# Routed experts: tokens fetched and results sent by indirect transfers, in place of products with a selection matrix, with the weights in rings of four buffers

## What is computed

```python
def moe_swiglu(x, router_w, router_b, w13, w2):
    t = x.reshape(b * n, d)
    logits = (t @ router_w).astype(jnp.float32) + router_b.astype(jnp.float32)
    probs = jax.nn.softmax(logits, axis=-1)
    top_p, top_i = lax.top_k(probs, TOP_K)
    top_p = top_p / jnp.sum(top_p, axis=-1, keepdims=True)
    gates = jnp.einsum('tk,tke->te', top_p, jax.nn.one_hot(top_i, N_EXPERTS, dtype=jnp.float32))
    out = jnp.zeros_like(t)
    for e in range(N_EXPERTS):
        out = out + gates[:, e:e + 1] * swiglu(t, w13[e], w2[e])
    return out.reshape(b, n, d)
# then: x = x + g2 * out; y = rmsnorm(x, final_norm)
```

## Time and profile before

| | us |
|---|---|
| median of 3 runs | 3472.29 (3462.05 to 3472.33) |
| the profiled execution | 3476.86 |
| its span, first to last instruction | 3475.1 |
| TensorE busy | 3105.1 |
| VectorE busy | 1412.7 |
| GpSimd busy | 1125.0 |
| ScalarE busy | 868.6 |

### The profile page before, as it was taken

One profiled execution on the slowest core, in us unless ns is written; L12 is line 12 of the kernel. 1 busy time (PEld: TensorE's weight loads), 2 busy tenths in 40 slices (PEclk: granted clock), 3 DMA queues, 4 the chain that ended last, 5 costly groups with the idle time before them and its releaser, 6 DMA issues.

```text
span 3475.1 us, 51066 instructions
## 1 busy us (share of the span) xinstructions
PE 3105.1 (89%) x20356; PEld 2801.9 (81%) x20356; DVE 1412.7 (41%) x1999; ACT 868.6 (25%) x1266; POOL 1125.0 (32%) x365
## 2 busy tenths in 40 slices
PE   7699888888888887899999896769999999999996
PEld 3499787777777775799999896768888888888895
DVE  0400246555654654421111406434444544453454
ACT  0200122322232222110010100123333334333432
POOL 1255022012202212456566454213323333332330
PEclk9799677677767866899999998869999999999997
DMA  9233211101110110122222121014545455454542
GB/s 297 84 128 107 70 34 55 40 24 45 39 48 21 54 51 26 49 61 83 57 74 72 57 82 51 10 49 128 145 139 163 137 142 155 139 139 145 161 137 71
DMA packets 427939, 309.93 MB, mean 89 GB/s; under 512 B 12145, under 2 KB 393066, under 8 KB 427882
## 3 DMA queue, kind: packets, MB, share of 16 engines
q1 hardware_dynamic: 414698, 286.08, 27.9%
q10 hardware_dynamic: 13184, 23.07, 1.9%
HBM read 294.96 MB, written 14.16 MB: 89 GB/s over the span
## 4 chain that ended last, share of the span: by engine, by line
PE 36%; issue 31%; POOL 12%; DVE 4%; ACT 2%; DMA 1%; DVEq 0%; POOLq 0%; SPq 0%; ACTq 0%
PE psum L542 15%; POOL m_lo L392 9%; PE psum L525 7%; PE psum L684 2%; PE psum L701 2%; PE psum L676 2%; POOL w_hi L433 2%; PE psum L691 2%; PE psum L590 2%; PE psum L707 1%; POOL w_lo L436 1%; DVE xt L1395 1%; PE psum L794 1%; ACT vn L1002 1%; PE psum L520 1%
## 5 line engine op out<-in xcount | busy, mean ns | idle before, releaser
L392 POOL TENSOR_TENSOR m_lo<-m_raw,m_hi 128x2048 fp32r<-128x2048 f32 (+1 forms) x81 | 357.3, 4411 | 724.9 <-ACT m_hi L1124 724.9
L778 PE MATMUL psum<-he_hi,m_hi 128*128 128x192 f32 x1584 | 444.1, 280 | 17.9 <-POOL m_lo L392 16.4
L433 POOL TENSOR_TENSOR w_hi<-raw,zero 128x2048 fp32r<-128x2048 f32 (+2 forms) x68 | 249.3, 3667 | 648.5 <-PE psum L542 549.4
L778 PE MATMUL psum<-he_lo,m_hi 128*128 128x192 f32 x1584 | 441.4, 279 | 0.0
L778 PE MATMUL psum<-he_hi,m_lo 128*128 128x192 f32 x1584 | 441.1, 278 | 0.0
L542 PE MATMUL psum<-a_hi,w_hi 128*128 128x320 f32 x1728 | 398.7, 312 | 42.8 <-DVE cy L1514 17.1
L542 PE MATMUL psum<-a_lo,w_hi 128*128 128x320 f32 x1728 | 397.6, 312 | 0.0
L542 PE MATMUL psum<-a_hi,w_lo 128*128 128x320 f32 x1728 | 397.1, 311 | 0.0
L469 POOL TENSOR_TENSOR ml<-lt,level 128x640 f32<-128x640 f32 x80 | 124.0, 1556 | 795.4 <-PE psum L525 795.1
L1124 ACT ACTIVATE m_hi<-m_raw 128x2048 fp32r<-128x2048 f32 (+1 forms) x164 | 290.5, 1772 | 345.6 <-DMA m_raw<-in_moe_w_dram 260.8
L436 POOL TENSOR_TENSOR w_lo<-raw,w_hi 128x2048 fp32r<-128x2048 f32 (+2 forms) x68 | 333.6, 4906 | 5.3
(11 more groups left out here) (297 smaller groups left out, 5217.5 us busy)
## 6 DMA issues: line engine op xcount, KB each, us to landing
m_raw<-in_moe_w_dram SPq DMA_DIRECT2D x274, 512.0 KB, 4.5
raw<-in_mod_w_dram SPq DMA_DIRECT2D x48, 512.0 KB, 3.9
raw<-in_ffn_w_dram SPq DMA_DIRECT2D x44, 512.0 KB, 4.7
mod_raw<-in_mod_w_dram SPq DMA_DIRECT2D x16, 1024.0 KB, 6.9
raw<-in_dn_w_in_dram SPq DMA_DIRECT2D x32, 512.0 KB, 4.5
m_raw<-in_moe_w_dram SPq DMA_DIRECT2D x54, 256.0 KB, 2.7
raw<-in_sc_w_in_dram SPq DMA_DIRECT2D x24, 512.0 KB, 4.1
projected<-stage ACTq DMA_DIRECT2D x16, 640.0 KB, 3.1
```

What stands on the lines that cost most here:

```text
L392: eng.tensor_tensor(m_lo[q][:, 0:n], m_raw[j % 2][:, 0:n], m_hi[q][:, 0:n].bitcast(F32), ALU.subtract)\
L433: pool.tensor_tensor(w_hi[s][:, 0:cols], raw[s][:, 0:cols], zero[:, :].broadcast_to([P, cols]), ALU.add)\
L778: mm = pe.matmul(psum[:, q, g * CAP:(g + 1) * CAP], w[:, c:c + P], v[:, k, :], start=(k == 0 and n == 0), stop=(k == KT - 1 and n == 2))
```

## The change

Nothing of what is computed changes. In the expert stage:

- `h_rows` in DRAM takes the normed tokens row by row. TensorE turns them back with 16 fp32r products for each of five tiles (high and low added in PSUM), ScalarE copies and sends them from its own queue. `xT` is turned back too, by 40 transposes, into `xtok2`.
- A table in DRAM has for each item and slot the token's row, the output row and the gate. GpSimd fills it with default entries (four `iota`, two memsets, two plain transfers of 16-byte pieces), VectorE computes `dest` and the gates by twelve small steps, GpSimd writes the entries by ten indirect transfers, waits, reads the whole table back (2880 pieces of 16 bytes in two plain transfers) and waits. Then it issues the first gather, sets `yb` to zero and gives the count that the first even weight loads wait for.
- In the loop GpSimd issues, before the low half of unit 10, two indirect transfers that send the previous item's output rows `yb` to `y_rows` and two that fetch the next item's token rows to `xg`. TensorE turns `xg` by 16 transposes at the place of the gather. Scatter, way back, `pick`, `back`, `y_hi`, `y_lo` and the additions to `xT` are gone; the output is scaled into `yb` by ScalarE alone.
- The weights have rings of four (`m_raw`, `m_hi`, `m_lo`); ScalarE makes high halves three units ahead. The down matrix is cut into nine units (seven single, two double), so an item has 20. An up unit is still three products of 192 for each tile, gate and up part now in different banks.
- At the end SyncE reads each token's two output rows (5 transfers of 1 MB); VectorE adds them, scales them by the gate row, adds `xtok2`; ScalarE makes sum of squares and root; VectorE scales; SyncE sends each tile.
- Several semaphores of earlier stages are merged; their waits stay as they are.

The diff, cut to its core:

```diff
-SLOTS = [(0, 0, P), (1, P, CAP - P)]
+PARTS = [(0, 0, P), (1, P, CAP - P)]
-DOWN_K = [(0, 1), (1, 1), (2, 1), (3, 2), (5, 2), (7, 2), (9, 2)]
+DOWN_K = [(k, 1) for k in range(7)] + [(7, 2), (9, 2)]
+RING = 4
+AHEAD = 3
...
@@ SyncE
+            for w in range(2):
+                sp.dma_start(g2_row[w].rearrange("(k p) -> p k", p=P), mod[:, 40:48, w],
+                             allow_slow_non_contiguous=True).then_inc(sem("g2_out"), 16)
...
+            def m_load(x, j, dst_src):
+                sp.wait_ge(sem(f"m_split{j % 2}"), x * (M_UNITS // 2) + (j // 2 + 1))
+                for dst, src in dst_src:
+                    sp.dma_start(dst, src).then_inc(sem(f"m_loaded{j % RING}"), 16)
...
@@ GpSimd
+            def gather_rows(idx):
+
+                for i, s0, ns in PARTS:
+                    pool.indirect_dma_start(xg[0:ns, i, :], None, h_rows[:, :],
+                                            bass.IndirectOffsetOnAxis(ap=idx[0:ns, i, 0:1].bitcast(I32), axis=0))\
+                        .then_inc(sem("rows_in"), 16)
...
+            pool.wait_ge(sem("dest"), 1)
+            for t in range(TT):
+                for r in range(2):
+                    pool.indirect_dma_start(table[:, :], bass.IndirectOffsetOnAxis(ap=dest[:, t, r:r + 1], axis=0),
+                                            entry[:, t, r, :], None).then_inc(sem("listed"), 16)
+            pool.wait_ge(sem("listed"), 16 * 2 * TT)
+            for i, s0, ns in PARTS:
+                pool.dma_start(tab2[0:ns, 1:MAX_ITEMS + 2, i, :], by_slot[s0:s0 + ns]).then_inc(sem("tabled"), 16)
+            pool.wait_ge(sem("tabled"), 32)
+            pool.wait_ge(sem("h_stored"), 16 * TT)
+            pool.wait_ge(sem("ht_t"), 2 * TT)
+            gather_rows(tab2[:, 1, :, :])
+            pool.memset(yb[:, :, :], 0.0).then_inc(sem("y_done"), 1)
+            pool.memset(small[:, 1, 0:1], 0.0).then_inc(sem("m_split0"), 2)
...
             with pool.Fori(0, n_items) as x:
                 for j in range(0, M_UNITS, 2):
+                    if j == 10:
+                        pool.wait_ge(sem("now"), x + 1)
+                        pool.nop(nofuse=True)
+                        scatter_rows()
+                        pool.wait_ge(sem("gathered"), x * 4 + 4)
+                        pool.nop(nofuse=True)
+                        gather_rows(now[:, 2, :, :])
                     m_low(pool, x, j)
...
@@ TensorE
-                pe.wait_ge(sem("picked"), x + 1)
+                pe.wait_ge(sem("rows_in"), x * 32 + 32)
                 for b in range(4):
                     for k in (2 * b, 2 * b + 1):
-                        for n, src in enumerate((ht_hi, ht_lo)):
-                            for t in range(TT):
-                                mm = pe.matmul(psum[:, b, (k % 2) * CAP:(k % 2 + 1) * CAP],
-                                               src[:, t, k * P:(k + 1) * P], pick[:, t, :],
-                                               start=(n == 0 and t == 0), stop=(n == 1 and t == TT - 1))
+                        for i, s0, ns in PARTS:
+                            mm = pe.transpose(psum[:, b, (k % 2) * CAP + s0:(k % 2) * CAP + s0 + ns],
+                                              xg[0:ns, i, k * P:(k + 1) * P], same[0:ns, 0, 0:ns])
                     mm.then_inc(sem("gathered"), 1)
...
-                    pe.wait_ge(sem(f"m_split{j % 2}"), x * (M_UNITS // 2) + (j // 2 + 2))
+                    pe.wait_ge(sem(f"m_split{j % 2}"), x * (M_UNITS // 2) + (j // 2 + 3))
...
@@ ScalarE
             def m_high(x, j):
-                act.wait_ge(sem("multiplied"), x * M_UNITS + (U_MOE + j - 2))
+                act.wait_ge(sem("multiplied"), x * M_UNITS + (U_MOE + j + 1 - RING))
...
+            for j in range(AHEAD):
+                m_high(0, j)
             gathered(0)
-            m_high(0, 0)
-            m_high(0, 1)
```

More of the change, by code:

```diff
@@ L81, in sem @@
             return sems[name]
+        with ExitStack() as tokens:
+            xg = sb("xg", [P, 2, D], F32, tokens)
+            yb = sb("yb", [P, 2, D], F32, tokens)
         xT = sb("xT", [P, KT, T])
@@ L201, in build @@
             m_sg = sb("m_sg", [P, CAP], F32, moe)
+            sb("m_gap6", [P, 3 * CAP], F32, moe)
             m_prod = sb("m_prod", [P, CAP], F32, moe)
[L203 to L214, removed]
+            xtok2 = sb("xtok2", [P, TT, D], F32, moe)
+            rows = sb("rows", [P, 3, D], F32, moe)
+            ident_r = sb("ident_r", [P, P], F32R, moe)
+            tab2 = sb("slot_tab", [P, MAX_ITEMS + 3, 2, 4], F32, moe)
+            entry = sb("entry", [P, TT, 2, 4], F32, moe)
+            dest = sb("dest", [P, TT, 2], I32, moe)
+            now = sb("now", [P, 3, 2, 4], F32, moe)
+            fin = sb("fin", [P, 3, TT], F32, moe)
+        he_hi, he_lo = he[:, :, 0, :], he[:, :, 1, :]
+        with ExitStack() as moe_rows:
+            sb("m_gap4", [P, 6 * UNIT + 4 * M_UNIT + 2 * KT * CAP], F32, moe_rows)
+            htok = sb("htok", [P, TT, D], F32, moe_rows)
+        with ExitStack() as moe_out:
+            sb("m_gap5", [P, 6 * UNIT], F32, moe_out)
+            yr = sb("yr", [P, TT, 2, D], F32, moe_out)
         psum = ctx.enter_context(nc.psum_tensor("psum", [P, 8, 512], F32))
@@ L357, in m_gated @@
+            with sp.Fori(0, n_items) as x:
                 e = sp.value_load(items[0:1, bass.ds(x, 1)], min_val=0, max_val=E - 1)
-                turn = x * (M_UNITS // 2)
                 src13 = w13_all[bass.ds(e * D, D), :].rearrange("(k p) m -> p k m", p=P)
[L360 to L363, removed]
@@ new lines, in _ @@
+            step(pool.memset(entry[:, :, :, :], 0.0))
+            for i in range(2):
+                step(pool.iota(tint[:, :, i, 1], pattern=[[0, MAX_ITEMS + 3]], base=2 * T + P * i, channel_multiplier=1))
+            step(pool.iota(eint[:, :, :, 0], pattern=[[P, TT], [0, 2]], base=0, channel_multiplier=1))
+            pool.iota(eint[:, :, :, 1], pattern=[[2 * P, TT], [1, 2]], base=0, channel_multiplier=2)\
+                .then_inc(sem("entries"), 1)
+            by_slot = table.rearrange("(x s) c -> s x c", s=CAP)
@@ L870, in _ @@
             mm.then_inc(sem("router_mm"), 1)
-            tokens_back(0, 5)
+            pe.wait_ge(sem("ident_r"), 1)
+            for t in range(TT):
+                if t >= 2:
+                    pe.wait_ge(sem("ht"), t - 1)
+                for k in range(KT):
+                    for n, src in enumerate((a_hi, a_lo)):
+                        mm = pe.matmul(psum[:, 4 + 2 * (t % 2) + k // 4, (k % 4) * P:(k % 4 + 1) * P],
+                                       src[:, k, t * P:(t + 1) * P], ident_r[:, :], start=(n == 0), stop=(n == 1))
+                mm.then_inc(sem("ht_t"), 1)
             pe.wait_ge(sem("sel"), 1)
@@ L1602, in _ @@
             dve.wait_ge(sem("items"), 1)
[L1603 to L1604 removed]
             n_items = dve.value_load(items[0:1, MAX_ITEMS + 1:MAX_ITEMS + 2], min_val=1, max_val=MAX_ITEMS)
[L1606 to L1615 removed]
+            dve.memset(small[:, 0, 0:1], 0.0).then_inc(sem("m_prod"), 1)
+            dve.memset(small[:, 2, 0:1], 0.0).then_inc(sem("m_split1"), 2)
             def gathered_low(x):
```

394 lines of the change are left out of this document (184 added, 210 removed).

## The result

The changed kernel takes 3234.3 us in the median (3224.3 to 3243.5), the kernel before 3467.2 with the runs made beside it. The ratio is 0.9329, 95% interval 0.9292 to 0.9366: 6.7% faster. The profiled execution, 3243.5 us with a span of 3241.7, is the slowest of its four. Its span is 233.4 us shorter than the one before.

The account below looks back on a forecast made before the run. It took the expert loop to be bound by TensorE's instructions. Span: 3475.1 - 246 (loop) + 24 (start) - 18 (tail) = 3235 us; adjusted from the profiled execution to the median, 3232; range 3200 to 3290.

Parts of the forecast that it names:

- the loop: Nine expert items, each falling from 119.3 to 92.0 us: 246 us off.
- the start: Start of the expert stage: count, table writes and reads, gather and weights put the first product 24 us later.
- the tail: From the last product to the end: 43.4 us after the change for 61.2, 18 less.
- the 0.7 us of seams: Allowance per loop item for the first double down unit and the seams, bringing 91.3 to 92.0 us.
- What bounds the kernel before: Expert loop: bound by TensorE's instructions, so their number matters; 114.6 us an item, the remaining 4.7 waits and drains.
- What hides GpSimd's transfers: Loop, before unit 10's low half: four indirect transfers at 1.2 us, 4.8 in all, hidden by 15.7 us of cover.
- Rival (b): Short start: ten table writes at 0.2 us, 10 less, and reads of 3 us, 14 less; 3208 us, chance 0.18.
- (a): Longer start: table writes and reads at upper bounds, slow clock, gathers; +56 less overlaps, about 3280 us; chance 0.13.
- (c): Loop: a low half, load or the four transfers late by 3 to 7 us an item; about 3280 us; chance 0.13.
- (d): Indirect transfers occupy GpSimd beyond their cover; gain gone at 8.2 us each, 3557 us at 10; chance 0.03.
- (e): Loop: weights set the pace; at 145 GB/s an item takes 130 us, the whole kernel 3574 us; chance 0.02.
- (f): Loop: freed of the products, but something unseen paces an item at 119 us; 3478 us; chance 0.01.

Follow-up runs that it names:

- e1: The changed kernel with the sixteen transposes of fetched rows grouped by form (128 or 64 rows): 3209.5 us.
- e9: The kernel before with the second transfer of each up unit cut to one eighth: 3422.6 us beside 3470.4.
- e3: The kernel before with 40 of the gather's 80 products an item left out: 3463.1 us against 3472.5, ratio 0.9986.
- e2: The changed kernel with weight loads waiting for the low half of two units before, not four; high halves still three ahead: 3380.6 us.
- e5: The changed kernel with twelve memsets of 512 columns an item on GpSimd ahead of its indirect transfers: 3239.1 us.
- e6: The changed kernel with 26 memsets of 512 columns an item on GpSimd ahead of its indirect transfers: 3327.5 us.
- e12: The changed kernel without VectorE's multiplication by the gate row at the end: 3224.4 us.
- e10: The kernel before with both the short up loads of e9 and the halved gather of e3: 3416.7 us beside 3470.4.
- e8: The changed kernel with grouped transposes, early count, and even weight loads released before GpSimd's table writes: 3198.1 us, ratio 0.9204.
- e4: The changed kernel with the two counting products moved ahead of the third of five turned tiles: 3222.1 us.

## Why the prediction was right, and where not

The time, 3232 for 3234, is partly luck. Two terms were off and went against each other: the loop saved 14 us less than counted, the start cost 6 less and the tail saved 1.5 more. That leaves 6.5 us too little saved, and the profiled execution, the slowest of its four, has a span of 3241.7 for the 3235 of the sum. The median lies closer because the runs spread.

**The loop** was to give 246 us and gave 232. The eleven up units (58.9 us) and the 132 down products (30.3) came as counted. The transposes were mis-sized: 1.8 us taken, 3.6 measured. I took the price from ten transposes that all read 128 rows; these alternate between 128 and 64, and e1 shows that the order makes the difference. The nine items, 845.9 us, are 18 above 9 x 92.0: 16 from the transposes, 6 from the clock behind them in four items (1.6 each), 3 from the low clock in the first units, less 7 for the 0.7 us of seams, which were not needed, and roundings. The loop before was 4 above 9 x 119.3, which makes 14.

**What bounds the kernel before** was only half right. I called the loop bound by the instructions that TensorE is given, so that what matters is how many of them go. e9 divides its item: of 119.3 us 114.3 are TensorE's own and 5.0 go with late weights. My sum had 114.6 and 4.7, and took 4.0 of the 4.7 off for the rings of four; it was right for that reason. But the number of instructions is not all that matters. In e3 40 us of them go and the time stays. In e2 all of them go, the loads start as late as before, and the loop takes 987.9 us for 845.9. Without the early loads the change is then worth 3472.5 - 3380.6 = 92 us of 238, with the reservation made at e2. The kernel before with rings of four was not run; e9's short loads, worth 48, stand in for it. Together these are 140, and the rest showed only with both.

**What hides GpSimd's transfers** was right, price and cover: 0.97 us of work each and 0.30 between them for 1.2 taken, hidden in every item. The low half behind them is ready 7.8 us before it is needed (in item two unit 10 starts at 2505.5, its low half is ready at 2497.7), and it had waited 0.7 us for ScalarE after the last transfer, so the cover left is 8.5, where my working leaves 15.7 - 4.8 = 10.9. GpSimd's low halves take 5.2 us there and not 4.6, and the high half is ready 13.0 us before its unit and not 14.2. e5 and e6 lie on both sides of it, and e6 puts it at 8.3.

**The start** was to cost 24 us and cost 18. The count came 9 us later, not 3.6: the clock stayed at 0.50 through all five tiles, 17.3 us, my upper bound. The destinations were ready at 2313.4 and not at 2307. The ten writes took 12.5 for 12.0. The reads of 2880 pieces, 17 taken, took 4.7 from issue to the first gather. Issuing the read of 1920 pieces takes GpSimd 1.26 us and that of 960 pieces 0.89, so 960 pieces more cost 0.37 us, where I had taken most of 1.2 for each 128. From the memset to the first product are 17.7 us for 18.4.

The Trainium skill (DMA: Bandwidth & Descriptors, "Anatomy of one DMA — SWDGE (gpsimd) path") calls the making of descriptors small, and in this the trace agrees. Its 2.0 us fixed per transfer stand beside landings of 2.1 us for the table writes, but 4.1 and 3.2 for the two reads. The some 6 us that the prediction drew from that page for writes and reads together were 18.9 (2313.4 to 2332.3): one indirect write after the other takes 0.97 us of GpSimd's time and 0.30 to the next. Rival (b) was thus right in its reads (3 us, 4.7 measured), wrong in its writes (2 us for ten, 12.5 measured), and the late count took another 5.

**The tail** was to save 18 and saved 19.5. The first of VectorE's passes starts 13.1 us after the last product for 12.2, and a pass is 1.25 for 1.3; e12 confirms that VectorE sets this stretch.

**The rivals.** (a), up to 56 us more at the start than counted, did not come: it cost 6 less. (c), waits in the loop, did not come; (d) needed 8.2 us for an indirect transfer and it is 0.97; (e) is refuted by 203 GB/s in the loop and 0.2 us of waiting for weights; (f) by items of 92.9 us.

## What to carry over

A busy share of 98% does not say that taking instructions away will pay: leave out a few, or shorten a load, and see which moves the item. If neither seems to, look where the idle time has come back, whether the kernel has a wait at that place, and what the clock did behind it; in e10 the answer lay there and not in the weights. Removing work and deepening a ring belong together where both bounds are close; one alone gives a part. Before a step is put on a queue, read off the trace how long what stands behind it is ready before it is needed; here some 8 us, and past it each microsecond cost 1.25 (e6), because the clock is low after the gap.

## What was not expected of the hardware

- Sixteen float32 transposes that read 128 and 64 rows in turn take 0.227 us each, grouped 0.117 (e1).
- After 3.6 us of alternating transposes the granted clock fell to 0.50 for 3.4 us in four of nine items, though TensorE had no gap; behind the grouped ones it held in all nine (e1).
- A plain transfer of 1920 pieces of 16 bytes cost GpSimd 1.26 us, one of 960 pieces 0.89, and an indirect one of up to 128 rows 0.97.
- Beside eight weight transfers the wait for ten small table writes was 6.25 us (e8), without them 1.70 and, with the same early count, 1.43 (e4).
- With 40 products fewer in its loop body TensorE stopped for 1.5 to 3.4 us after the seventh product of each new round, with no semaphore to wait for (e10). The cause is open.
